# Value products of a chunked linear-attention layer: one fp32 product as three fp32r products of high and low parts

## What is computed

```python
dmat = jnp.where(order, b[..., :, None] - b[..., None, :] + ig[..., None, :], -jnp.inf)
m_t = jnp.maximum(inter, jnp.max(dmat, axis=-1))
s = jnp.einsum('bhtd,bhsd->bhts', q, k) * jnp.exp(dmat - m_t[..., None])
num = a[..., None] * jnp.einsum('bhtd,bhde->bhte', q, C) + jnp.einsum('bhts,bhse->bhte', s, v)
den = a * jnp.einsum('bhtd,bhd->bht', q, n) + jnp.sum(s, axis=-1)
h = num / jnp.maximum(jnp.abs(den), jnp.exp(-m_t))[..., None]
```

## Time and profile before

| | |
|---|---|
| runs | 2988.45 us median (2986.16 to 2990.36) |
| span of the profiled execution | 2986.1 us |
| PE busy | 2929.7 us, 98% |
| DVE busy | 2084.4 us, 70% |
| ACT busy | 1176.1 us, 39% |
| POOL busy | 104.3 us, 3% |
| mean granted PE clock | 0.998 of 2.4 GHz |

### The profile page before, as it was taken

One profiled execution on the slowest core, in us unless ns is written; L12 is line 12 of the kernel. 1 busy time (PEld: TensorE's weight loads), 2 busy tenths in 40 slices (PEclk: granted clock), 3 DMA queues, 4 the chain that ended last, 5 costly groups with the idle time before them and its releaser, 6 DMA issues.

```text
span 2986.1 us, 43506 instructions
## 1 busy us (share of the span) xinstructions
PE 2929.7 (98%) x17066; PEld 2341.7 (78%) x17066; DVE 2084.4 (70%) x3947; ACT 1176.1 (39%) x2054; POOL 104.3 (3%) x188
## 2 busy tenths in 40 slices
PE   8999999999999999999999999999999999999989
PEld 6777778888888888878887877888888888885346
DVE  4576876788888776676676886677675678765455
ACT  4322323322232232242235555455444445543344
POOL 0000000000000000000000000000010120000000
PEclk9999999999999999999999999999999999999999
DMA  9778784354555455538736774645676453487997
GB/s 381 275 267 290 267 283 142 126 169 149 190 168 177 162 183 169 180 126 274 239 120 209 255 237 139 201 148 180 195 239 218 140 166 127 152 274 260 401 404 314
DMA packets 193197, 641.69 MB, mean 215 GB/s; under 512 B 21488, under 2 KB 36192, under 8 KB 192992
## 3 DMA queue, kind: packets, MB, share of 16 engines
q1 hardware_dynamic: 132080, 423.44, 40.6%
q10 hardware_dynamic: 58032, 207.12, 20.5%
q0 software_dynamic: 2880, 8.35, 0.9%
HBM read 624.15 MB, written 12.58 MB: 213 GB/s over the span
## 4 chain that ended last, share of the span: by engine, by line
PE 87%; DVE 6%; DMA 3%; ACT 2%; issue 1%; SPq 1%; DVEq 0%; POOL 0%; ACTq 0%; POOLq 0%
PE PS L503 15%; PE PS L499 11%; PE PS L501 9%; PE PS L502 9%; PE PS L632 8%; PE PS L634 8%; PE PS L633 8%; PE PS L1058 2%; PE PS L795 2%; DMA AR<-e_w 1%; PE PS L1466 1%; DVE WL L2383 1%; PE PS L1435 1%; PE PS L1422 1%; PE PS L1116 1%
## 5 line engine op out<-in xcount | busy, mean ns | idle before, releaser
L2383 DVE TENSOR_TENSOR WL<-WR,WH 128x1024 fp32r<-128x1024 f32 (+1 forms) x566 | 682.7, 1211 | 402.1 <-ACT WH L1568 400.6
L503 PE MATMUL PS<-HT,WL 128*128 128x256 f32 (+1 forms) x2928 | 952.2, 325 | 0.0
L1568 ACT ACTIVATE WH<-WR 128x1024 fp32r<-128x1024 f32 (+1 forms) x566 | 587.0, 1044 | 871.3 <-PE PS L503 481.1
L503 PEld LDWEIGHTS PS<-HT,WL 128*128 128x128 f32 x2928 | 552.6, 189 | 48.3 <-issue 0.5
L499 PE MATMUL PS<-HT,WH 128*128 128x512 f32 x1584 | 566.0, 401 | 9.1 <-DVE WL L2383 6.0
L501 PE MATMUL PS<-HT,WH 128*128 128x512 f32 (+1 forms) x1344 | 519.0, 386 | 5.0 <-DVE HT L2363 2.4
L502 PE MATMUL PS<-HT,WH 128*128 128x512 f32 (+1 forms) x1344 | 508.5, 378 | 0.0
L632 PE MATMUL PS<-WH,HT 128*128 128x512 f32 x1016 | 408.1, 402 | 3.6 <-DVE HT L2363 2.5
L634 PE MATMUL PS<-WH,HT 128*128 128x512 f32 x1016 | 396.4, 390 | 0.0
L633 PE MATMUL PS<-WL,HT 128*128 128x512 f32 x1016 | 395.6, 389 | 0.0
L499 PEld LDWEIGHTS PS<-HT,WH 128*128 128x128 f32 x1584 | 297.3, 188 | 89.6 <-issue 13.7
(11 more groups left out here) (467 smaller groups left out, 3284.3 us busy)
## 6 DMA issues: line engine op xcount, KB each, us to landing
WR<-ada_w SPq DMA_DIRECT2D x264, 512.0 KB, 4.7
AR<-e_w SPq DMA_DIRECT2D x88, 512.0 KB, 10.0
E_RING<-e_w SPq DMA_DIRECT2D x80, 512.0 KB, 10.4
WR<-m_vo ACTq DMA_DIRECT2D x64, 512.0 KB, 4.4
WR<-a_qz ACTq DMA_DIRECT2D x64, 512.0 KB, 4.8
WR<-n_m SPq DMA_DIRECT2D x64, 512.0 KB, 4.4
AR<-ada_p ACTq DMA_DIRECT2D x56, 512.0 KB, 6.4
AR<-ada_p SPq DMA_DIRECT2D x48, 512.0 KB, 8.7
```

The source lines that it names most:

```text
L503: return e.matmul(ps[:, 0:b - a], wl, HH_[:, c, a:b], start=False, stop=c == last)
L1568: e.activation(part_of(WH, s), place_of(plan["slot"][p])[:, 0:width(s)], ACT.Copy, scale=1.0).then_inc(*L.up(hi_done, ("hi", s)))
L2383: e.tensor_tensor(part_of(WL, s), place_of(plan["slot"][plan["split"][s]])[:, 0:width(s)], part_of(WH, s).bitcast(F32), ALU.subtract).then ...
```

## The change

1. Each value product becomes three fp32r products: high P by high V, high P by low V, low P by high V, of 258 columns (two columns of ones instead of one).
2. ACT copies the high part of P into `M_PH` after tt(k), and the high part of V into `M_VH` at the end of vo. DVE subtracts: `lows(k)` writes the low part of P over P (`M_PL` is the place of `M_P`) after tt(k+1) or, for k = 3, after one of the two half blocks of `bg`; `M_VL` takes the place of the copy to `M_V`.
3. The parts of P that no product reads are no longer computed: `M_USED` gives 2688 of the 3072 columns.
4. `bg(2)` behind tt(3) becomes `bg(1)`, `lows(3)`, `bg(1)`.
5. The new tiles need 12 KB of each partition. They come from the descriptor space, which shrinks from 16 to 4 KB. `ARR` is a second name for the arena, as fp32r.

```diff
-NAR = 10272
+NAR = 13344
-    AR = sb("AR", [128, NAR])
+    with ExitStack() as plain:
+        AR = plain.enter_context(nc.sbuf_tensor("AR", [128, NAR], F32))
+    ARR = sb("ARR", [128, NAR], F32R)
...
-    M_V = cv(4 * 257, "p (t n) -> p t n", t=4)
+    cv(4 * 258)
...
+    M_VH, M_VL = (ARR[:, at:at + 1032].rearrange("p (t n) -> p t n", t=4) for at in (2048, 11784))
+    M_PH = [ARR[:, 8712 + 1536 * d:10248 + 1536 * d] for d in range(2)]
+    M_PL = [ARR[:, 5128 + 1536 * d:6664 + 1536 * d] for d in range(2)]
...
+    M_USED = {(0, 0): (0, 512), (0, 1): (0, 512), (1, 0): (128, 512), (1, 1): (0, 512),
+              (2, 0): (0, 256), (2, 1): (0, 128), (3, 0): (128, 256), (3, 1): (0, 256)}
...
-                            w.wait_ge(L.at(("p", h, k, d), ("ve", h), ("one", "v")))
-                            i = e.matmul(ps[:, 0:257], M_P[d][:, c:c + 128], M_V[:, k, :], start=m == 0,
-                                         stop=m == len(ks) - 1)
+                            ph, pl = M_PH[d][:, c:c + 128], M_PL[d][:, c:c + 128]
+                            w.wait_ge(L.at(("p", h, k, d), ("ve", h)))
+                            e.matmul(ps[:, 0:258], ph, M_VH[:, k, :], start=m == 0, stop=False)
+                            e.matmul(ps[:, 0:258], ph, M_VL[:, k, :], start=False, stop=False)
+                            i = e.matmul(ps[:, 0:258], pl, M_VH[:, k, :], start=False, stop=m == len(ks) - 1)
...
                 for tb in range(4):
+                    e.activation(M_VH[:, tb, 0:256], place[("vo", h, tb)][:, 0:256], ACT.Copy, scale=1.0).then_inc(
+                        *L.up(act_done, ("vh", h, tb)))
                     e.activation(M_O[:, tb, :], place[("vo", h, tb)][:, 256:512], ACT.Tanh, scale=0.5).then_inc(
...
                 for k in range(4):
+                    for d in range(2):
+                        at = m_span(k, d)[0]
+                        w.wait_ge(L.at(("pp", h, k, d)))
+                        e.activation(M_PH[d][:, at], M_P[d][:, at], ACT.Copy, scale=1.0).then_inc(
+                            *L.up(act_done, ("ph", h, k, d)))
                     if k == 0 and h:
                         z_(2 * h)
...
-                    w.wait_ge(L.at(("oe", h, tb)))
-                    copy(M_V[:, tb, 0:256], place[("vo", h, tb)][:, 0:256], ("ve", h), ("free", ("vo", h, tb)))
+                    w.wait_ge(L.at(("vh", h, tb), ("oe", h, tb)))
+                    tt(M_VL[:, tb, 0:256], place[("vo", h, tb)][:, 0:256], M_VH[:, tb, 0:256].bitcast(F32), ALU.subtract,
+                       ("ve", h), ("free", ("vo", h, tb)))
...
+                def lows(k):
+                    for d in range(2):
+                        at = m_span(k, d)[0]
+                        w.wait_ge(L.at(("ph", h, k, d)))
+                        tt(M_PL[d][:, at], M_P[d][:, at], M_PH[d][:, at].bitcast(F32), ALU.subtract, ("p", h, k, d))
+
                 for k in range(4):
+                    if k:
+                        lows(k - 1)
                     for d in range(2):
...
-                        tt(p, p, place[("S", h, k)][:, 0:512 - c0], ALU.mult, ("p", h, k, d), ("free", ("S", h, k)))
+                        tt(p, p, place[("S", h, k)][:, s], ALU.mult, ("pp", h, k, d), ("free", ("S", h, k)))
...
                     elif k == 3 and h < 7:
                         along(("k", h + 1))
-                        bg(2)
+                        bg(1)
+                lows(3)
+                if h < 7:
+                    bg(1)
...
-    nc = _bacc.Bacc("TRN2", target_bir_lowering=False, num_devices=1)
+    nc = _bacc.Bacc("TRN2", target_bir_lowering=False, num_devices=1, dynamic_dma_scratch_size=4096)
```

More of the change, by code:

```diff
@@ L196, in _program, with m_span @@
     M_PC = [0, 512, 1024, 1280]
+    M_USED = {(0, 0): (0, 512), (0, 1): (0, 512), (1, 0): (128, 512), (1, 1): (0, 512),
+              (2, 0): (0, 256), (2, 1): (0, 128), (3, 0): (128, 256), (3, 1): (0, 256)}
+    def m_span(k, d):
+        a, b = M_USED[k, d]
+        return slice(M_PC[k] + a, M_PC[k] + b), slice(a, b)
     M_KEYS = {0: ([0], [0, 1]), 1: ([0, 1], [1]), 2: ([0, 1, 2], [0, 1, 2, 3]), 3: ([0, 1, 2, 3], [0, 1, 3])}
@@ L1880, in vo @@
                     w.wait_ge(L.at(("o_used", h - 1)))
+                    w.wait_ge(L.at(("v_used", h - 1)))
                 for tb in range(4):
+                    e.activation(M_VH[:, tb, 0:256], place[("vo", h, tb)][:, 0:256], ACT.Copy, scale=1.0).then_inc(
+                        *L.up(act_done, ("vh", h, tb)))
                     e.activation(M_O[:, tb, :], place[("vo", h, tb)][:, 256:512], ACT.Tanh, scale=0.5).then_inc(
@@ L1902, in mlstm @@
                 for k in range(4):
-                    n = 512 if k < 2 else 256
                     for d in range(2):
-                        p = M_P[d][:, M_PC[k]:M_PC[k] + n]
+                        p = M_P[d][:, m_span(k, d)[0]]
                         w.wait_ge(L.at(("pt", h, k, d)))
@@ L2836, in mlstm @@
             scaled(M_HN, M_HN, 0.5, ALU.mult)
-            e.memset(M_V[:, :, 256:257], 1.0).then_inc(*done(("one", "v")))
             along(("first", 1))
@@ L2891, in vo @@
                     w.wait_ge(L.at(("v_used", h - 1)))
+                else:
+                    one = ONE[:, 0:8].rearrange("p (t n) -> p t n", t=4)
+                    copy(M_VH[:, :, 256:258], one)
+                    tt(M_VL[:, :, 256:258], one, one, ALU.subtract)
                 for tb in range(4):
-                    w.wait_ge(L.at(("oe", h, tb)))
-                    copy(M_V[:, tb, 0:256], place[("vo", h, tb)][:, 0:256], ("ve", h), ("free", ("vo", h, tb)))
+                    w.wait_ge(L.at(("vh", h, tb), ("oe", h, tb)))
+                    tt(M_VL[:, tb, 0:256], place[("vo", h, tb)][:, 0:256], M_VH[:, tb, 0:256].bitcast(F32), ALU.subtract,
+                       ("ve", h), ("free", ("vo", h, tb)))
             def along_vo(h, first):
@@ L2914, in mlstm @@
                     for d in range(2):
-                        p = M_P[d][:, M_PC[k]:M_PC[k] + 512 - c0]
-                        ts(p, place[("cb", h, d)][:, c0:512], M_ACOL[:, k, 32 * d + h:32 * d + h + 1], 0.0,
+                        at, (a, b) = m_span(k, d)[0], M_USED[k, d]
+                        p = M_P[d][:, at]
+                        ts(p, place[("cb", h, d)][:, c0 + a:c0 + b], M_ACOL[:, k, 32 * d + h:32 * d + h + 1], 0.0,
                            ALU.add, ALU.min, ("pt", h, k, d), *([("free", ("cb", h, d))] if k == 3 else []))
+                def lows(k):
[3 more added lines that the diff above has]
+                        tt(M_PL[d][:, at], M_P[d][:, at], M_PH[d][:, at].bitcast(F32), ALU.subtract, ("p", h, k, d))
                 for k in range(4):
+                    if k:
+                        lows(k - 1)
                     for d in range(2):
-                        c0 = 0 if k < 2 else 256
-                        p = M_P[d][:, M_PC[k]:M_PC[k] + 512 - c0]
+                        at, s = m_span(k, d)
+                        p = M_P[d][:, at]
                         w.wait_ge(L.at(("pa", h, k, d), ("full", ("S", h, k))))
-                        tt(p, p, place[("S", h, k)][:, 0:512 - c0], ALU.mult, ("p", h, k, d), ("free", ("S", h, k)))
+                        tt(p, p, place[("S", h, k)][:, s], ALU.mult, ("pp", h, k, d), ("free", ("S", h, k)))
                     if k == 0 and h:
```

## The result

The changed kernel takes 2995.55 us (median; 2994.8 to 3000.17) against 2988.45 us: ratio 1.0027, 95% interval 1.0017 to 1.0036. It is slower: the interval does not reach 1, though the amount is at the edge of what a measurement of this kernel can tell. The time lies inside the predicted range, 5.0 us above the forecast and 1.1 us above the band that the prediction called the same (2982.5 to 2994.4, chance 0.69). The profiled execution has a span of 2993.8 us against 2986.1.

What follows compares the result with a forecast made beforehand. PE was taken to bound the kernel, except behind DVE's arrival at tile 1 in heads 0 to 4. Terms +0.8, +1.7, -2.5 and +1.9 sum to +1.9 us, giving 2990.5 us; range 2985 to 3001.

Steps and rivals of the forecast that it cites:

- What bounds the kernel: Whole kernel: PE's work bounds it, but in heads 0 to 4 DVE's arrival at tile 1 sets the value products' end.
- PE's own work: Value products: fp32r pitch 0.1208 us, sixty take 7.25 us instead of 8.52, 1.27 us less in a head.
- The copy ahead of tanh: End of vo: ACT does eight short instructions instead of four, some 1.2 us more, costed at 0 to 0.1 us a head.
- the walk: Head 1, DVE's steps to tile 1: arrival at 734.9 instead of 733.57, 1.33 us late; such a head changes by +0.43 us.
- The idle 3.16 us: Head 1, DVE's wait before its last cut behind tt(3): takes up most of the delay, 0.77 us left.
- Heads 5 and 6: DVE arrives when tile 1 is full, so PE is the bound: -1.27 us each.
- Head 0: No z(0), so tt(0), lows(0), tt(1) follow each other; DVE reaches tile 1 1.75 us later, head +0.8 us.
- Head 7: Nothing lies between DVE's steps: 6.2 us to tile 1, arrival 1309.4 instead of 1306.0; +1.9 us, 0.7 either way.
- The clock as a rival: Heads 0 to 4: the new 2.5 us stop costs PE its clock, 3.1 us each, 2998 to 3007; chance 0.15.
- Late weight pieces: Rival: cuts for q and k, 2.4 and 2.6 us ahead, come late; 14 us for each us over; chance 0.09.
- slow products: Rival: fp32r at 258 columns runs no faster than fp32's records, +34 us, 3024; chance 0.03 together with descriptor space.
- descriptor space: GpSimd's DMAs with a quarter of the space: cost 0, at most some us; chance 0.03 together with slow products.

Runs made afterwards that it cites:

- e1: Changed kernel with tanh ahead of the copy of V's high part on ACT at the end of vo: 2996.6 us, ratio 1.0022 to the kernel before.
- e9: Changed kernel, tanh ahead of V's high-part copy, both half blocks behind tt(3) moved to the next vo's second and fourth piece: 2980.77 us, ratio 0.9969.
- e6: Kernel before with descriptor space of 4 KB, wider arena and the unread columns of P not computed: 2989.15 us, ratio 1.0000.
- e11: Kernel before with only the half blocks behind tt(3) moved to the second and fourth piece of vo: 2986.84 us, ratio 0.9996.
- e3: Changed kernel with eight idle fp32 products between tiles 4 and 5 in heads 1 to 4: 2997.72 us, ratio 1.0026 to the kernel before.
- e10: Changed kernel, tanh first, doubled half blocks at vo's second, fourth and sixth piece, none behind its last in heads 1 to 4: 2982.95 us, ratio 0.9982.
- e5: Changed kernel with one fp32 value product of the high parts instead of three fp32r, low parts still made: 3008.16 us, ratio 1.0061.
- e12: Changed kernel with only the half blocks moved to vo's second and fourth piece, tanh still behind the copy: 2983.97 us, ratio 0.9979.

## Why the prediction was right or wrong

- **What bounds the kernel.** Right. In heads 1 to 4 DVE's arrival at tile 1 set the end, and PE's saving on the first four tiles became a stop: 2.94, 2.52, 2.56 and 2.55 us where 2.5 was predicted, and 1.93 in head 0.
- **PE's own work.** Right: pitch 0.120 us (0.1208 predicted), 1.30 us a head. It missed 0.2 us a head for the change of type between fp32 products and vo.
- **The copy ahead of tanh (0 to 0.1 us a head).** This is the term that failed. It is 1.28 us, and since the walk has no slack, it goes on to tile 1: e1 took 1.08 us off the arrival. With e1's order heads 2 to 4 arrive at 49.60 us, half a microsecond before the 50.1 of the walk; with the load, half a microsecond after. So the walk's other steps were costed about 0.5 us too long, and the load was left out. That the stop is 2.5 us all the same is luck: the products, too, start 0.42 us later than before, behind the late z.
- **The idle 3.16 us that should take up most of the delay.** DVE's wait before the last cuts is 1.44 us now. But it is ACT's copy of P and cut, which themselves wait for DVE's tt(3), so nothing is taken up any more. Timeline of ACT of after, head 1:

```profile
726.59 0.75 ACT L1928 ACTIVATE ARR<-AR 128x128 fp32r<-128x128 f32 x2 [5.21 <-DVE AR L2375]
...
727.25 2.00 ACT L1582 ACTIVATE WH<-WR 128x1024 fp32r<-128x1024 f32 x2
```

  Head 1, with 0.4 us of extra work near its start, arrives 0.44 us later than head 2; in before both arrived together.
- **Heads 5 and 6.** Predicted -1.27, measured -1.09 and -1.13: -1.3 for the products and -0.2 for the type, +0.4 for the late z.
- **Head 0.** Predicted +0.8, measured -0.18. DVE's arrival moved by 0.87 us and not by 1.75. The forecast gives this walk without its steps, so which of them was costed too high stays open.
- **Head 7.** Predicted +1.9, measured +4.18. Timelines of DVE and PE of after:

```profile
1309.43 1.29 DVE L2375 TENSOR_TENSOR ARR<-AR,ARR 128x512 fp32r<-128x512 f32 x2
...
1315.96 0.15 DVE L2384 SCALAR_TENSOR_TENSOR SML<-PS,SML 128x1 f32<-128x1 f32 x1
```

```profile
1311.83 1.22 PE L1053 MATMUL PS<-AR 128*128 128x256 f32 x2 [3.62 <-DVE AR L2375]
...
1322.33 0.40 PE L513 MATMUL PS<-HT,WH 128*128 128x512 f32 x1
```

  From lows(0) to tile 1 is 6.53 us, where 6.2 was predicted. But the walk began at the old gate's end, 13.47 us behind S(0), and in after lows(0) starts 15.12 us behind it: the load and ACT's copy ahead of the cuts, which I had put into head 1 and left out here. S(3) waits 3.62 us where the earlier trace rows has 1.31. The clock was down too, but tile 5 had to wait for DVE in any case (0.15 us).
- **The clock as a rival.** I gave it 0.15, and it came true in the size of two heads: 1.4 us each in heads 1 and 4, not the 3.1 of its own estimate, since in head 1 the records were back at 0.28 from 740.52 us on. Two heads of five was the rival's own condition, with 6.2 us for the two; they cost 2.7. The prediction held it unlikely because the clock had stayed at 1.00 behind the stop of 2.37 us at 2893.97. That row was one execution: seven of the thirteen later traces have the same stop of 2.37 us ahead of the same products, and in four of the seven the clock fell behind it. e9's timeline and window:

```profile
2885.76 5.35 PE L1480 MATMUL PS<-E_DYN,E_HID 128*32 128x256 f32 x64 [2.37 <-ACT HT L2325]
```

```profile
2885.00:2890.00 5.00, 4.24 (x52) 2.84 (x56) 2.79 (x8) 2.07 (x8) 0.00 (x0) 0.71 1.03 409
```

  The Trainium skill (TensorE: Matmul & The Clock Gate, A second HAM failure mode: psum-queue depth-cycling) describes another kernel, with bf16 matmuls of 512 columns, whose short idle times between groups of matmuls, while it cycles through PSUM banks, make the clock go up and down. The stops here are of that kind, a wait for a PSUM bank, but come once a head; that the clock fell and came back in four heads in a row of e1 is in line with it.
- **Late weight pieces, slow products, descriptor space.** None came: no product waits for a low part in the layer's waits of after, the products' pitch is 0.120 us, and in e6 the smaller space, with the unread columns left out, changes nothing that can be measured.

The differences from the predicted change are -1.0 in head 0, +2.2, +0.4, +0.4 and +1.8 in heads 1 to 4, +0.3 in heads 5 and 6, +2.3 in head 7: together 6.5 us. The clock is 2.7 of it; the rest is the load, less what the walk had over-costed, and head 7's start.

That the time fell inside the range is in part luck. With all terms at their high ends the prediction had +7, 2995.5 us. The layer alone took 8.4 us more, and it is the 1.1 us less behind the layer, which no term forecast, that brought the kernel back to this; the rest of the range, up to 3001, was room for the clock and for late pieces. Three of the prediction's sums do not come out as written. Its low end takes two thirds of the 8 us from 2990.5, but the 8 us are counted from the kernel before: 2983, not 2985. The clock's times count the 1.9 us twice: 2988.45 + 8 and + 17 are 2996.5 and 3005.5, not 2998 and 3007. And 34 us on 2988.45 are 3022.5, not 3024. None of these changes the account above.

## What to carry to other kernels

When an instruction is put ahead of a step that waits, ask what else hid in that wait: here a table load that no source line shows. A faster engine gains only as far as the work that feeds and drains it keeps up, so look at what DVE still has to do before it can empty the first bank, and move work that can wait out of that stretch, to where its own loads have arrived and nobody waits for DVE. e9 did this and put tanh first, and the same products went from 0.3% slower to 0.3% faster; the move alone, in the kernel before (e11), could not be told from no change. Before a new stop is costed at its length, look whether PE comes out of it at full clock, and do not settle that by one row of one trace: the same stop in the same instructions went both ways here.

## What the runs showed of the hardware

- Stops of 2.29, 1.88, 1.86 and 1.86 us, each behind 2.1 us of products, brought the half clock in heads 1 to 4 of e1. Stops of 2.5 to 2.6 us in after did so once in three heads, one of 2.94 us did, and one of 1.92 us did in e3 and, as 1.93 us, not in after and e1. The length alone does not decide it in these rows, and what does stays open. A fall behind such a stop cost 1.4 to 1.7 us.
- The granted clock fell also behind the layer, where the kernels run the same instructions, at places that differ from kernel to kernel (1505, 2153, 2310 and 2887 us in e9; 1510, 1950, 2315 and 2892 us in e10). From the end of head 7 to the end of the span it took from 1671.5 us (after) to 1676.1 (e5), so a gain under some 3 us is better read from the layer's length than from the median, and only in heads that are alike from trace to trace.
- The first fp32r product of vo starts its successor 0.43 us later when fp32 products stand ahead of it (e5), 0.23 us when fp32r ones do (after).
- A table load of 1.28 us costs nothing when the function that needs it is the first instruction behind a wait (before, e1), and stands on the path when a copy of the same result is ahead of it (after, e12).
